# A residual block with forgetting attention: who issues the forget-row loads, where four weight splits stand, and where two output projections begin

## The chip, the cores and the metric

The kernel runs on one core of one Trainium2 chip. The metric is the device time of one execution in microseconds (us), median of the runs. Five engines work side by side: PE (TensorE, matmuls), DVE (VectorE), ACT (ScalarE), POOL (GpSimd) and SP (SyncE, which here only issues DMAs). Each takes its instructions strictly in order; they meet through semaphores, and a wait holds back everything behind it on the same engine.

## The reference, cut to what matters

```python
h = rms_norm(x, g1);  z = h @ w_in                  # x: 512 tokens x 1024 channels
q, k = rms_norm(q), rms_norm(k)                      # per head, 8 heads of 64
F = cumsum(log_sigmoid(z_f + b))                     # forget rows, one per head
s = q @ k.T * d**-0.5 + F[t] - F[s], causal;  y_attn = softmax(s) @ v
y_pool = pool_scale * ((trailing_mean(z_pool, w) - z_pool) @ w_pool[g])   # w = 2, 4, 8, 16
x = x + concat[y_pool, y_attn] @ w_out               # the mixer stage ends here
x = x + peer_ffn(rms_norm(x, g2))                    # 128 x 128 experts, top 16 of 8 heads
```

## The kernel before

**Layout.** Channels lie on the 128 partitions, the 512 tokens along the free dimension. Every weight block is one of a numbered list n = 0, 1, 2, ...: 0 to 3 are the value projections, 4 is the forget projection (`F_W`), 5 to 12 the query and key projections (`QK_W`), 13 to 16 the pool projections (`POOL_W`), 17 to 24 the output projections (`OUT_W`), 25 to 28 four early expert blocks (`EARLY_W`), and from 29 on the retrieval queries and the experts.

**A weight's way.** Matmuls are made in pairs of parts, high and low, so each block is loaded by SP into one of three buffers `raw` (L392), ACT copies the high part to `wh` (`hi_to`, L438, called "split n" below), POOL subtracts to get the low part `wl` (L411), and PE's projection n (`project`, L620 to L622, 24 matmuls of 512 columns) waits for `w_lo`. SP may load block n once the low part of n - 3 is done; ACT may split n once projection n - 4 has used its buffer. In the mixer stage ACT calls `hi_to(n + 3)` at projection n, just before it copies that projection's result to `zc` (L473). The first norm calls `hi_to` at k = 1 and k = 7 (splits 0 and 1), its second half at k = 0 and 4 (splits 2 and 3). The second norm has split 28 at k = 4; splits 29 to 32 come in the stage after it.

**The order of the mixer stage** is written out by hand in `stages`, one list that PE follows with what stands inside each projection, and that ACT and DVE follow flattened (`in_turn`). `head(h, n, more)` stands for the transposes of head h's probabilities, projection n, and inside it at given k: the sums of squares and norm of an earlier q or k (`ss`, `norm`), the four score blocks of head h + 1 (`score`, PE L705; DVE L1017 to L1022; ACT's exponential L491) and their scaling (`scale`, L1030), and head h's last transposes. `pv` is the product with the values. Each head has one forget row, broadcast over the partitions into `nf[h % 2]`, which DVE adds to the scores (L1019).

**The forget rows** come from DVE's scan (L960, semaphore `f_done`). SP stores them to memory (L372), waits for the store, and loads row h with `nf` (L379) ahead of weight block `SCORED[h]` + 1, that is ahead of blocks 9, 10, 12, 13, 14, 15, 16 and 17. For h of 2 and more it first waits for `s_masked` = 4(h - 1): that the last score block of head h - 2 has been masked by DVE, since this frees the buffer.

**Pool mixing.** DVE makes the trailing mean of group g (`mean`, L984 to L1001), PE multiplies it by `w_pool` (`poolmix`, L695), ACT and DVE store high and low parts to `hh` and `hl` (L486, L1005). All four products use one bank, `bank[SS]`, so a poolmix waits for the one before to be stored (`pool_lo`).

**The end of the stage.** Output projection 17 has the order k = 4, 5, 6, 0, 1, 2, 3, 7, as the pool parts (k below 4) and the last pair of heads (k = 7) come last. Each output projection is added to x by DVE (L965), and its square sum is taken one projection later (L635).

## Time and profile before

| what | us |
|---|---|
| runs shown: median (lowest to highest) | 1580.68 (1578.74 to 1581.0) |
| the profiled execution: its own time | 1589.65 |
| its span, first to last instruction | 1587.8 |
| PE busy, share of the span | 1521.5, 96% |
| DVE busy | 1148.2, 72% |
| POOL busy | 973.5, 61% |
| ACT busy | 604.8, 38% |

In the profile a row of an engine's timeline is "start us, duration us, engine, line, instruction, count", and in brackets how long the engine had been idle before it and what ended that idle time. PE is drawn as busy over nearly the whole span, but in the first 300 us, the mixer stage and the second norm, its slices show seven to eight tenths, and the granted TensorE clock is below full speed in several of them. From there to the end the slices are at nine tenths and more.

### The profile page before, as it was taken

How to read it: one execution, taken by the hardware profiler on the slowest of the kernel's cores; microseconds unless marked ns; L12 is line 12 of the kernel's file. 1: busy time of each engine (PE TensorE's matmuls, PEld its weight loads, DVE VectorE, ACT ScalarE, POOL GpSimd, SP SyncE). 2: the span in 40 equal slices, each digit the busy share in tenths (PEclk: the TensorE clock that was granted, in tenths of full speed). 3: DMA queues.
4: the chain of work that ended last, by engine and by line, in shares of the span. 5: the costliest groups of instructions: out<-in, count | busy, mean ns of one | idle time of the engine just before them, and what ended most of it. 6: DMA issues, size and time to landing. Idle time of an engine off the chain costs nothing.

```text
span 1587.8 us, 20624 instructions
## 1 busy us (share of the span) xinstructions
PE 1521.5 (96%) x7613; PEld 1326.5 (84%) x7613; DVE 1148.2 (72%) x1938; ACT 604.8 (38%) x808; POOL 973.5 (61%) x525
## 2 busy tenths in 40 slices
PE   7888889899999999999999999999999999999999
PEld 4654557788999999999999999998888888888887
DVE  5565572416699999928898889938777777777774
ACT  5565433433333333343343334433333333333332
POOL 2411113333468788667666676658787878878784
PEclk9998899999999999999999999999999999999999
DMA  4211212222347777658989988799889888888983
GB/s 152 94 40 40 79 41 80 99 81 80 113 168 267 266 255 269 216 174 303 346 310 355 363 337 317 254 325 392 338 336 350 319 349 318 345 343 326 349 303 119
DMA packets 117973, 381.52 MB, mean 240 GB/s; under 512 B 11416, under 2 KB 27928, under 8 KB 117408
## 3 DMA queue, kind: packets, MB, share of 16 engines
q1 hardware_dynamic: 71264, 204.76, 35.5%
q0 software_dynamic: 36864, 134.23, 23.1%
q10 hardware_dynamic: 9792, 41.95, 6.6%
q8 instruction: 18, 0.29, 0.1%
q14 instruction: 35, 0.29, 0.0%
HBM read 336.84 MB, written 44.06 MB: 240 GB/s over the span
## 4 chain that ended last, share of the span: by engine, by line
PE 81%; DVE 6%; DMA 5%; ACT 4%; issue 2%; POOL 1%; SPq 0%; ACTq 0%; DVEq 0%
PE bank L620 25%; PE bank L621 25%; PE bank L622 24%; PE bank L809 5%; DMA picked<-u_dram,picks 3%; DMA raw<-wst_dram 2%; PE bank L753 1%; POOL wl L411 1%; DVE zc L933 1%; ACT wh L438 1%; DVE rinv L916 1%; PE bank L705 1%; ACT L509 1%; PE bank L635 1%; ACT L511 0%
## 5 line engine op out<-in xcount | busy, mean ns | idle before, releaser
L411 POOL TENSOR_TENSOR wl<-raw,wh 128x1024 fp32r<-128x1024 f32 x211 | 521.3, 2472 | 488.4 <-ACT wh L438 487.3
L620 PE MATMUL bank<-hh,wh 128*128 128x384 f32 (+1 forms) x1184 | 427.0, 361 | 4.2 <-POOL wl L411 4.2
L621 PE MATMUL bank<-hl,wh 128*128 128x384 f32 (+1 forms) x1184 | 414.1, 350 | 0.0
L622 PE MATMUL bank<-hh,wl 128*128 128x384 f32 (+1 forms) x1184 | 413.9, 350 | 0.0
L438 ACT ACTIVATE wh<-raw 128x1024 fp32r<-128x1024 f32 x225 | 237.0, 1054 | 172.3 <-PE bank L622 138.9
L621 PE MATMUL bank<-wl,Wh 128*128 128x512 f32 x768 | 300.7, 392 | 0.0
L620 PE MATMUL bank<-wh,Wh 128*128 128x512 f32 x768 | 300.0, 391 | 0.0
L622 PE MATMUL bank<-wh,Wl 128*128 128x512 f32 x768 | 298.4, 389 | 0.0
L620 PEld LDWEIGHTS bank<-hh,wh 128*128 128x128 f32 x1184 | 224.7, 190 | 14.1 <-issue 6.2
L621 PEld LDWEIGHTS bank<-hl,wh 128*128 128x128 f32 x1184 | 224.8, 190 | 9.6 <-issue 1.7
L622 PEld LDWEIGHTS bank<-hh,wl 128*128 128x128 f32 x1184 | 224.0, 189 | 8.9
L421 POOL DMA_INDIRECT picked<-v_dram,picks x128 | 195.3, 1526 | 24.9 <-issue 22.2
L1046 DVE SCALAR_TENSOR_TENSOR junk<-picked,wide 128x1024 bf16<-128x1024 f32 x128 | 155.2, 1213 | 25.2 <-DMA picked<-u_dram,picks 23.1
L620 PEld LDWEIGHTS bank<-wh,Wh 128*128 128x128 f32 x768 | 144.2, 188 | 31.8
L622 PEld LDWEIGHTS bank<-wh,Wl 128*128 128x128 f32 x768 | 144.2, 188 | 31.1
L621 PEld LDWEIGHTS bank<-wl,Wh 128*128 128x128 f32 x768 | 144.3, 188 | 29.2
L1173 DVE SCALAR_TENSOR_TENSOR wide<-picked,pick_a,wide 128x1024 f32<-128x1024 f32 x128 | 163.7, 1279 | 0.5
L411 POOL TENSOR_TENSOR wl<-xraw,wh 128x1024 fp32r<-128x1024 f32 x54 | 131.3, 2432 | 49.9 <-ACT wh L438 49.3
L438 ACT ACTIVATE wh<-xraw 128x1024 fp32r<-128x1024 f32 x72 | 76.7, 1066 | 198.2 <-PE bank L622 182.9
L560 ACT ACTIVATE act_a<-bank 128x384 f32<-128x384 f32 x124 | 61.1, 493 | 232.5 <-PE bank L622 224.7
L421 POOL DMA_INDIRECT picked<-u_dram,picks x128 | 125.4, 979 | 30.3 <-issue 19.6
L1152 DVE TENSOR_TENSOR oh<-bank,slotT 128x1024 f32<-128x1024 f32 x96 | 117.4, 1223 | 34.8 <-ACT bank L577 31.2
(164 smaller groups left out, 1767.2 us busy)
## 6 DMA issues: line engine op xcount, KB each, us to landing
raw<-uT_dram SPq DMA_DIRECT2D x128, 512.0 KB
xraw<-v_dram SPq DMA_DIRECT2D x72, 512.0 KB
raw<-v_dram SPq DMA_DIRECT2D x56, 512.0 KB
a_dram<-act_a ACTq DMA_DIRECT2D x64, 384.0 KB
wf<-a_dram SPq DMA_DIRECT2D x32, 768.0 KB, 6.9
raw<-wst_dram SPq DMA_DIRECT2D x41, 512.0 KB
gates_dram<-gbuf ACTq DMA_DIRECT2D x4, 4096.0 KB, 16.6
gt<-gates_dram SPq DMA_DIRECT2D x32, 512.0 KB
```

Of the source, the lines that this page charges most:

```text
L411: pool.tensor_tensor(wl[:, n % SPLIT, :], raw_of(n), wh[:, n % SPLIT, :].bitcast(F32), ALU.subtract).then_inc(w_lo, 1)
L421: pool.indirect_dma_start(out=picked[:, j % ROWS, :], out_offset=None, in_=u if j < PICKS else v_rows, in_offset=bass.IndirectOffsetOnAxis ...
L438: act.activation(wh[:, n % SPLIT, :], raw_of(n), ACT.Copy).then_inc(w_hi, 1)
L509: act.activation(root[:, :], var[:, :], ACT.Ln).then_inc(ln_ready, 1)
L560: act.activation(a_of(j), bank[n % 2][:, 0:DT], ACT.Gelu).then_inc(out_done, 1)
L620: pe.matmul(dst, ah, bh, start=start, stop=False)
L621: pe.matmul(dst, ah, bl, start=False, stop=False)
L622: return pe.matmul(dst, al, bh, start=False, stop=stop)
L809: last = pe.matmul(bank[GP + of % 2][:, t * P:(t + 1) * P], oh[:, of % 2, 1, t, :], oh[:, of % 2, 0, t, :], start=True, stop=True)
L1046: dve.scalar_tensor_tensor(junk[:, :], picked[:, j % ROWS, :], 1.0, wide[:, :], ALU.mult, ALU.mult, accum_out=pick_a[:, j:j + 1]).then_inc ...
L1152: step(dve.tensor_tensor(oh[:, s], bank[IOTA_BANK][:, 0:P].unsqueeze(1).unsqueeze(1).broadcast_to(both), slotT[:, 0:2, at].unsqueeze(3).br ...
L1173: dve.scalar_tensor_tensor(wide[:, :], picked[:, j % ROWS, :], pick_a[:, i:i + 1], wide[:, :], ALU.mult, ALU.add).then_inc(first_added, 1)
```

## The change

- SP no longer stores or loads the forget rows. ACT does: it waits for `f_done` and issues the store between the copy of projection 5 to `zc` and its square; it waits for the store and issues the rows of heads 0 and 1 in the same place of projection 6; and after the last exponential of head h it issues the row of head h + 2, with no wait of its own.
- ACT splits weight 1 at k = 4 of the first norm and weight 2 at k = 7; weights 28, 29 and 30 at k = 0, 3 and 6 of the second.
- `begin` is new: the nine matmuls of k = 4, 5, 6 of output projections 17 and 18 are issued before poolmix 2 and after mean 3. The projections then run k = 0, 1, 2, 3, 7.
- poolmix 1 moves from k = 6 to k = 0 of projection 16, ahead of head 7's scores.

```diff
-        stages += head(6, POOL_W + 3, (6, "mean", 2), (6, "poolmix", 1)) + [("pv", 6, [])]
-        stages += [("poolmix", 2, []), ("transpose", (7, 0), []), ("transpose", (7, 1), []), ("mean", 3, [])]
-        stages += [("transpose", (7, 2), []), ("pv", 7, []), ("poolmix", 3, [])]
+        stages += head(6, POOL_W + 3, (0, "poolmix", 1), (6, "mean", 2)) + [("pv", 6, [])]
+        stages += [("begin", OUT_W, []), ("poolmix", 2, []), ("transpose", (7, 0), []), ("transpose", (7, 1), [])]
+        stages += [("mean", 3, []), ("begin", OUT_W + 1, []), ("transpose", (7, 2), []), ("pv", 7, [])]
+        stages += [("poolmix", 3, [])]
...
+        BEGUN, LEFT = (4, 5, 6), (0, 1, 2, 3, 7)
...
-                if n == SCORED[0] + 1:
-                    sp.wait_ge(f_done, 1)
-                    sp.dma_start(f_dram, fg[:, 2, :]).then_inc(f_stored, 16)
-                    sp.wait_ge(f_stored, 16)
-                for h in range(HEADS):
-                    if n != SCORED[h] + 1:
-                        continue
-                    if h >= 2:
-                        sp.wait_ge(s_masked, TB * (h - 1))
-                    sp.dma_start(nf[:, h % 2, :], f_dram[h:h + 1, :].broadcast_to([P, T])).then_inc(nf_in[h % 2], 16)
...
+            def forget(h):
+
+                act.dma_start(nf[:, h % 2, :], f_dram[h:h + 1, :].broadcast_to([P, T])).then_inc(nf_in[h % 2], 16)
+
...
-                        if k in (1, 7):
-                            hi_to(k // 7)
+                        if k in (1, 4, 7):
+                            hi_to(k // 3)
...
+                        if n == QK_W[0]:
+                            act.wait_ge(f_done, 1)
+                            act.dma_start(f_dram, fg[:, 2, :]).then_inc(f_stored, 16)
+                        elif n == QK_W[1]:
+                            act.wait_ge(f_stored, 16)
+                            for h in range(2):
+                                forget(h)
...
+                    if b == TB - 1 and h + 2 < HEADS:
+                        forget(h + 2)
...
-                        if what == "norm2" and k in (0, 4):
-                            hi_to(EARLY_W + 2 + k // 4)
+                        if what == "norm2" and k in (0, 3, 6):
+                            hi_to(EARLY_W + 3 + k // 3)
...
+            def free_bank(n):
+
+                if bank_of(n) in last_in_bank:
+                    pe.wait_ge(*taken(last_in_bank[bank_of(n)]))
+                last_in_bank[bank_of(n)] = n
...
+                    begun = n in (OUT_W, OUT_W + 1)
                     project(bank[bank_of(n)][:, :], n % SPLIT, *((hh, hl) if kd == "out" else (mh, ml)), between,
-                            (4, 5, 6, 0, 1, 2, 3, 7) if n == OUT_W else range(KD))
+                            LEFT if begun else range(KD), first=BEGUN[0] if begun else 0)
...
+                elif what == "begin":
+                    pe.wait_ge(w_lo, i + 1)
+                    free_bank(i)
+                    project(bank[bank_of(i)][:, :], i % SPLIT, hh, hl,
+                            lambda k: pe.wait_ge(att_lo, 2 * (k - 4) + 2), BEGUN, first=BEGUN[0])
```

## Rows read from the trace of the kernel before

**Rows 1.** Chain that ended last, first 300 us, shares of the whole span by line:

```profile
by line: PE bank L620 8.6%; DMA raw<-wst_dram 8.3%; PE bank L621 8.0%; PE bank L622 8.0%; issue 7.2%; DVE zc L933 3.7%; DVE rinv L916 3.2%; PE bank L705 3.0%; ACT L509 3.0%; PE bank L635 2.8%; ACT L511 2.6%; DVE pr L1019 2.5%; DVE pad L989 
```

**Rows 2.** Waits, 120 to 190 us: who <- for whom, us in total, times, longest:

```profile
ACT wh L438 <- DMA raw<-wst_dram: 18.1, 4, 5.4
```

**Rows 3.** Waits of SP's queue, first 300 us, same columns:

```profile
SPq L379 <- DVE nmax L1022: 111.0, 6, 23.4
```

**Rows 4.** Timeline of SP's queue, one of six such pairs:

```profile
144.54 0.33 SPq L379 DMA_DIRECT2D nf<-forget_dram  x1
144.91 0.43 SPq L392 DMA_DIRECT2D raw<-wst_dram  x1
```

**Rows 5.** Timeline of ACT: one split, last exponentials of heads 5, 6 and 7:

```profile
149.64 1.06 ACT L438 ACTIVATE wh<-raw 128x1024 fp32r<-128x1024 f32 x1 [4.28 <-DMA raw<-wst_dram]
...
180.51 0.72 ACT L491 ACTIVATE pr<-pr,nmax 128x512 f32<-128x512 f32 x1 [0.81 <-DVE nmax L1022]
...
199.14 0.72 ACT L491 ACTIVATE pr<-pr,nmax 128x512 f32<-128x512 f32 x1 [4.28 <-DVE nmax L1022]
...
214.03 0.73 ACT L491 ACTIVATE pr<-pr,nmax 128x512 f32<-128x512 f32 x1 [2.07 <-DVE nmax L1022]
```

**Rows 6.** Windows: length, busy PE, PEld, DVE, ACT, POOL, granted clock, DMA, GB/s:

```profile
126.14:144.54 18.40, 13.94 (x46) 7.93 (x47) 9.66 (x31) 10.37 (x19) 2.35 (x1) 0.91 0.13 43
...
155.00:164.00 9.00, 9.00 (x17) 4.80 (x16) 6.67 (x23) 4.83 (x12) 0.00 (x0) 0.50 0.02 8
```

**Rows 7.** Timeline of PE: scores of heads 6 and 7, poolmix 2:

```profile
182.69 0.92 PE L705 MATMUL bank<-kn,qn 64*128 64x128 f32 x4
...
205.74 0.92 PE L705 MATMUL bank<-kn,qn 64*128 64x128 f32 x4
...
222.06 1.84 PE L695 MATMUL bank<-pm,wp 128*128 128x512 f32 x2 [4.05 <-DVE hl L1005]
```

**Rows 8.** Timeline of DVE: means 1 and 2, first steps of poolmix 0 and 1, x of projection 18:

```profile
200.60 0.42 DVE L984 COPY pad<-zc 128x512 f32<-128x512 f32 x1
...
205.58 0.74 DVE L1005 SCALAR_TENSOR_TENSOR hl<-bank,vec,hh 128x512 fp32r<-128x512 f32 x1
...
215.49 0.42 DVE L984 COPY pad<-zc 128x512 f32<-128x512 f32 x1
...
221.17 0.74 DVE L1005 SCALAR_TENSOR_TENSOR hl<-bank,vec,hh 128x512 fp32r<-128x512 f32 x1
...
242.20 0.69 DVE L965 TENSOR_TENSOR x<-x,bank 128x512 f32<-128x512 f32 x1 [2.92 <-PE bank L622]
```

**Rows 9.** Timeline of PE: first matmuls of projections 1, 3 and 4:

```profile
24.98 0.80 PE L620 MATMUL bank<-wh,hh 128*128 128x512 f32 x1 [2.93 <-POOL wl L411]
...
39.41 0.50 PE L620 MATMUL bank<-wh,hh 128*128 128x512 f32 x1 [0.32 <-POOL wl L411]
...
46.81 0.50 PE L620 MATMUL bank<-mh,wh 128*128 128x512 f32 x1 [1.19 <-POOL wl L411]
```

**Rows 10.** Timeline, DVE's scan and PE's first two sums of squares of q and k:

```profile
58.27 3.25 DVE L960 TENSOR_TENSOR_SCAN fg<-fg 8x512 f32<-8x512 f32 x1
59.43 1.10 PE L635 MATMUL bank<-sq,cst 128*128 128x512 f32 x2 [1.44 <-ACT sq L443]
...
70.73 2.04 PE L635 MATMUL bank<-sq,cst 128*128 128x512 f32 x2 [4.72 <-ACT sq L443]
```

**Rows 11.** Timeline, second norm: ACT's split 28, DVE's last parts, PE's projection 29:

```profile
294.75 1.06 ACT L438 ACTIVATE wh<-raw 128x1024 fp32r<-128x1024 f32 x1 [0.76 <-DVE zc L933]
...
300.95 1.48 DVE L869 TENSOR_TENSOR hl<-zc,hh 128x512 fp32r<-128x512 f32 x2
...
307.02 0.47 PE L620 MATMUL bank<-hh,wh 128*128 128x512 f32 x1 [4.22 <-POOL wl L411]
```

**Rows 12.** Timeline of ACT and of its queue, early expert blocks:

```profile
304.72 1.06 ACT L438 ACTIVATE wh<-raw 128x1024 fp32r<-128x1024 f32 x1
304.86 0.34 ACTq L531 DMA_DIRECT2D a_dram<-act_a  x1
```

## What the change will do to the time, predicted before it ran

> **What bounds the kernel now.** I read the slices of the page first: from about 300 us on PE is at nine tenths and above, so an edit of the first 300 us acts by how much earlier the retrieval queries start, and the rest moves along with them. I find no wait there that this change touches. Then the chain that ended last, for those 300 us. Three PE lines of the projections hold most, but the fourth entry is the transfer of weight blocks, 8.3% [rows 1]. So PE is not the only bound here. The waits say whose it is: from 120 to 190 us ACT stands four times before split 14, 15, 16 and 17 for a transfer, 18.1 us in all, 5.4 the longest [rows 2]. Why is the transfer late? SP stood 111.0 us before its loads of forget rows, on DVE's mask [rows 3], and the weight load is issued right behind: row at 144.54, block 15 at 144.91 [rows 4], split at 149.64 after 4.28 of idling [rows 5]. Its buffer had been free for long. Two heads, from the mask at 144.54 to the last exponential of head 5 at 180.51, take 35.97 us, 18.0 each [rows 4, 5].
>
> **Part 1, the rows on ACT's queue, heads 3 to 5.** SP now waits only for a free buffer, so blocks 14 to 17 are there long before they are split, and the four waits go. What is late next? In a head's 18.4 us PE is busy 13.9 at a mean clock of 0.91, DVE 9.7, ACT 10.4 [rows 6]. PE's work at full clock is 13.9 x 0.91 = 12.7. Without its wait a head takes 18.0 - 4.3 = 13.7 (splits, copies, table loads, exponential, DVE's norm steps, the next scores, one after another). That is still above 12.7, so the chain through ACT and DVE stays the bound, by 1 us, and three waits come back whole: 18.1 - 5.35 = **-12.8**.
> The rows themselves: each is issued behind an exponential of 0.72 us [rows 5] and takes ACT's sequencer 0.34. The trace has such an issue on ACT, at 304.86, beside a split that started at 304.72 [rows 12]: the engine doesn't stop. I take 0; were none hidden, 6 x 0.34 = 2.0. What the row waits for, the mask, the exponential ahead of it has waited for already, and it is wanted over a head's time later, so its own transfer is covered.
>
> **Head 6.** Its scores start at 182.69, behind transposes that wait for DVE, which stays so. From there PE ran into 5.35 us of waiting and then half clock. Head 7's scores started at 205.74 with PE never idle, and the exponential came 8.3 us later, at 214.03 [rows 5, 7]. By that pattern head 6's comes at 182.69 + 8.3 = 191.0, not 199.14 [rows 5]: **-8.2**, of which 5.35 is the wait and the rest clock.
>
> **Head 7, with poolmix 1 moved ahead of its scores.** It needs mean 1 and the stored parts of poolmix 0. DVE needs 205.58 - 200.60 = 5.0 for the mean [rows 8] and starts it 1.5 after the exponential: 191.0 + 1.5 + 5.0 + 0.7 = 198.2. PE gets there at 195.7: after the exponential it still has 1.7 of projection and poolmix 0, the value product (2.16) and the transposes (0.86), 4.7 in all. So it stands 2.5, where before it never stood. Head 7's last exponential follows 0.45 + 8.3 later, 206.95, a period of 16.0 for 14.9: **+1.1** (0 if the mean comes sooner, +3.5 if the stand drops the clock).
>
> **The tail.** Before: exponential 214.03 to x of projection 18 at 242.20, 28.2 [rows 5, 8], with PE idle 4.05 before poolmix 2 alone [rows 7], as poolmix 1's parts were stored only at 221.9 [rows 8]. After, from 206.95: value product until 210.0, begin 17 (9 matmuls, 0.233 from one start to the next at full clock, 2.1) until 212.1. Poolmix 2 waits for mean 2, 1.5 + 5.7 [rows 8] after the exponential, 214.2. Transposes to 215.6, begin 18 to 217.7, the last transposes and value product to 220.8; mean 3 (4.5) ends at 221.2; poolmix 3; then 15 + 15 matmuls, 7.0, end at 228.9: 22.0. **-6.2**. The 18 matmuls moved are 4.2 of it; the others are poolmix 1's earlier store. Poolmix 2 and mean 3 keep a stand of 2.0 and 0.4. Bounds: -3 (half clock after these stands) to -8.
>
> **Part 2, splits 1 and 2 earlier.** Projection 1 started at 24.98, waiting for POOL; now at 22. But projection 3 waits for split 3, which doesn't move (39.41), and projection 4 for split 4 (46.81) [rows 9]. So nothing is gained, and the idle time gathers before projection 3: 39.4 - 22 - 2 x 5.5 = 6.4 us. After the 2.9 us at 24.98 two projections took 14.1 us for 11, as the clock fell [rows 9]: a loss of 3.1, unseen then. It now falls in projection 3, with 1.2 us of slack behind it: +1.9 (0 to +4). The split inside the norm's alternation of ACT and DVE costs 0.3 (0 to 1.06).
>
> **Part 3, the store of the rows on ACT.** The wait for the scan stands between the copy of projection 5 and its square; behind it on ACT are the square, the root of that norm, split 9, and POOL, PE and DVE wait for those. The scan ends at 61.5, the square's sum ran on PE at 59.43 [rows 10]. Now it is 61.5 + 0.34 + 0.65, near 62.6: +3.1, with PE idle 4.7. Against it, PE's idle of 4.72 before the next sum at 70.73 [rows 10] goes for the most part (ACT stood for block 9, held on SP by the rows). The two idles change places, one projection earlier, each with a spell of half clock behind it. Following kn to the first scores I get -1.0 for the pair. Parts 2 and 3 together: **+1.2**, with bounds -2.5 and +5.
>
> **Part 4, second norm.** Before, projection 29 waited for POOL until 307.02, 4.22 us, since its split came only after the norm [rows 11]. Now splits 28 to 30 stand in the norm. Each takes 1.06 in a gap of 0.76 [rows 11], so 0.3 late, and at k = 0 there is no gap, 1.0; less the old one, 1.3 in all. The norm's last low part was done at 302.4 [rows 11], so projection 29 starts near 303.7: **-3.3** (-1.5 to -4.2). What now ends last is DVE's norm.
>
> **Sum.** 1.2 - 12.8 - 8.2 + 1.1 - 6.2 - 3.3 = **-28.2 us**. The profiled execution took 1589.65 with a span of 1587.8, which the sum makes 1559.6; the median of the runs shown is 9 below it, and the difference lies outside the stage. 1580.7 - 28.2 = **1552.5**.
>
> **A rule against it.** SP's queue shows that the weight load was held by a wait of 111.0 us, not by transfers: a row and a block are issued 0.37 us apart [rows 3, 4]. That speaks for order, not bandwidth, as the bound.
> The Trainium skill (DMA: Bandwidth & Descriptors, section Issuing engines are not separate DMA queues) states that DMAs from several engines share the same 16 DMA engines, and that spreading them saves only the issue time. By that rule alone the first rival below is the outcome, 1571. I hold that the rule tells of transfers, not of the in-order wait in front of them.
>
> **Rivals.**
> *Only the issues come back (0.03).* If the blocks were late for transfer time rather than for SP's place, part 1 returns 6 x 0.37 = 2.2 [rows 4] for 21, and the sum is -9: 1571. For it: a block needs 4.7 us to land [rows 4, 5]. Against: by the code its buffer was block 12's, split a whole head before, and the DMA share is 0.13 [rows 6].
> *The clock takes part of it (0.22).* PE's margin per head is 1 us; in 155 to 164 us it was at 0.50 with PE busy throughout [rows 6]. One head at half clock lasts about as long as 12.7 / 0.5 = 25.4 by PE alone, partial spells cost 2 to 4 each; two or three of them at head 7's poolmix, in the tail and at the start: 1556 to 1563.
> *No spells at all (0.20).* Heads packed closer leave PE little idle, projections 3 and 6 run at full clock: 1546 to 1550.
> *Slower (0.02).* If tight heads leave PE just idle enough to be held at the half level from head 2 to head 7, a head takes 25.4 for 13.7, 11.7 more. From 28.2 / 11.7 = 2.4 such heads on the change loses; with four it ends at 1580.7 - 28.2 + 46.8 = 1599. Against: the fuller heads of now (199 to 214) ran at full clock nearly throughout.
> *Forecast, 1550 to 1556 (0.53).*
>
> **Range and chances.** The range 1545 to 1562 holds the forecast, the case without spells and most of the case with them. About 0.2%, 3.2 us, is what a measurement of this kernel can tell from no change. All cases but the slower one lie beyond it on the fast side, less 0.01 for two heads at half clock, which end near no change: faster 0.97, same 0.01, slower 0.02.
>
> **What would show it.** Right: no row "ACT wh <- DMA raw" after 72 us; a head's period near 13.8; SP waiting on POOL only; PE idle about 2.5 before poolmix 1 and 2 before poolmix 2; projection 29 started by DVE's last `hl`, some 28 us before 307. Wrong: first sum of squares of q not 3 us late (part 3), projection 4 within 0.5 of 46.8 (part 2), heads of 15 us and more with PE as the releaser or half clock (the margin of 1 us), ACT idle behind a row's issue.

## The result and the profile after

The changed kernel takes 1562.78 us (median of 6 runs, 1558.53 to 1571.51), the kernel before took 1580.84 beside it (6 runs, 1578.74 to 1584.26). The ratio is 0.9894, with a 95% interval of 0.9872 to 0.9916: 1.1% faster, some 17 to 18 us, where 28.2 were forecast. The median lies 0.8 us above the top of the range.

The profiled execution of after took 1571.51, with a span of 1569.7, against 1589.65 and 1587.8. Both profiles lie about 9 us above their medians, so they can be set side by side. The page of after:

```profile
PE 1513.6 (96%) x7613; PEld 1323.5 (84%) x7613; DVE 1156.7 (74%) x1938; ACT 602.9 (38%) x808; POOL 973.6 (62%) x525
```

From 1587.8 to 1569.7 PE gave back 8 us of busy time, with the same matmuls: that is clock (mean granted clock 0.983, before 0.978). DVE's busy time has **risen** by 8.5 us, though it has no new work. That line is the first trace of what I missed.

The same points of the stage in both traces give the shift of each stretch, to be set against the forecast. Each step is the change of one stretch, in us:

| stretch, its end before → after | before | after | measured | forecast |
|---|---|---|---|---|
| start to projection 4, 46.81 → 47.02 | 46.81 | 47.02 | +0.2 | +2.2 |
| to exponential of head 0, 88.82 → 89.65 | 42.01 | 42.63 | +0.6 | -1.0 |
| heads 1 and 2, 126.14 → 126.95 | 37.32 | 37.30 | 0.0 | 0 |
| heads 3 to 5, 180.51 → 168.17 | 54.37 | 41.22 | -13.15 | -12.8 |
| head 6, 199.14 → 182.13 | 18.63 | 13.96 | -4.7 | -8.2 |
| head 7, 214.03 → 198.78 | 14.89 | 16.65 | +1.8 | +1.1 |
| tail, to x of projection 18, 242.20 → 222.99 | 28.17 | 24.21 | -4.0 | -6.2 |
| x of projection 18 to x of 24, 280.92 → 261.71 | 38.72 | 38.72 | 0.0 | 0 |
| second norm, to projection 29, 307.02 → 288.01 | 26.10 | 26.30 | +0.2 | -3.3 |
| from there to the end of the span | 1280.8 | 1281.7 | +0.9 | 0 |

So 19.0 of 28.2 arrived at projection 29. The waits show that part 1 did what was said. SP's queue, first 300 us, against the 111.0 on DVE in [rows 3]; the same view of ACT from 120 to 200 us holds no wait of `wh` for a transfer, against [rows 2]:

```profile
SPq L382 <- POOL wl L401: 278.9, 33, 17.4
```

The last exponentials of heads 2, 5, 6 and 7 in ACT's timeline, with the issue of a forget row beside one of them (against [rows 5]):

```profile
126.95 0.72 ACT L492 ACTIVATE pr<-pr,nmax 128x512 f32<-128x512 f32 x1 [0.81 <-DVE nmax L1037]
...
168.17 0.72 ACT L492 ACTIVATE pr<-pr,nmax 128x512 f32<-128x512 f32 x1 [0.81 <-DVE nmax L1037]
168.18 0.33 ACTq L437 DMA_DIRECT2D nf<-forget_dram  x1
...
182.13 0.72 ACT L492 ACTIVATE pr<-pr,nmax 128x512 f32<-128x512 f32 x1 [3.84 <-DVE nmax L1037]
...
198.78 0.72 ACT L492 ACTIVATE pr<-pr,nmax 128x512 f32<-128x512 f32 x1 [2.07 <-DVE nmax L1037]
```

Head 2's, at 126.95, is the point from which the three heads are counted. All six such issues (heads 0 to 5) stand beside the exponential, 0.33 us beside 0.72, and cost nothing, as [rows 12] had it. Windows of after, with the columns of [rows 6]: head 5, head 6, head 7, the tail, and the second norm.

```profile
154.78:168.17 13.39, 13.05 (x53) 7.95 (x52) 9.67 (x31) 9.60 (x19) 2.35 (x1) 1.00 0.17 59
168.17:182.13 13.96, 12.10 (x42) 7.23 (x41) 10.26 (x31) 5.75 (x14) 2.38 (x1) 0.81 0.18 58
182.13:198.78 16.65, 15.49 (x58) 9.34 (x57) 12.36 (x34) 7.37 (x16) 2.67 (x1) 0.95 0.09 32
198.78:222.99 24.21, 21.42 (x84) 15.56 (x83) 15.86 (x28) 9.31 (x15) 5.30 (x3) 0.93 0.12 44
264.28:288.01 23.73, 16.61 (x96) 16.29 (x95) 19.27 (x22) 12.00 (x16) 7.29 (x3) 0.96 0.14 47
```

Heads 3 to 5 run at full clock and take 14.05, 13.77 and 13.39 us. From head 6 on the clock is below it, and DVE has more busy time than its steps need: 10.26 in head 6 against 8.19 before.

**Where the rest went.** The chain that ended last, in after, goes through one long piece in head 6 (start, length, what):

```profile
170.08 2.86 DVE pad L1004
```

and the timeline around it:

```profile
170.01 2.38 POOL L401 TENSOR_TENSOR wl<-raw,wh 128x1024 fp32r<-128x1024 f32 x1 [11.04 <-ACT wh L428]
170.08 2.85 DVE L1004 TENSOR_TENSOR pad<-pad 128x512 f32<-128x512 f32 x1
...
175.54 0.88 PE L720 MATMUL bank<-kn,qn 64*128 64x384 f32 x2 [1.65 <-DVE nmax L1037]
```

One addition of mean 0 takes 2.85 us. In before the same addition took 0.69:

```profile
182.42 0.69 DVE L989 TENSOR_TENSOR pad<-pad 128x512 f32<-128x512 f32 x1
...
187.81 2.34 POOL L411 TENSOR_TENSOR wl<-raw,wh 128x1024 fp32r<-128x1024 f32 x1 [16.48 <-ACT wh L438]
```

The difference is what POOL does meanwhile. In after it subtracts block 17 from 170.01 to 172.39, and DVE's step, begun 0.07 later, ends 0.5 behind it (172.93). In before split 17 was late for its transfer, so POOL came at 187.81, when all of mean 0 was over. This was my theory after the result, **A**: a DVE step that reads two operands from SBUF stands until a running subtraction of POOL ends. The early splits, which part 1 makes possible and part 4 orders, put POOL's subtractions on top of such steps. The Trainium skill (SBUF — State Buffer, section Who interferes with whom) states this: a DVE instruction with two SBUF inputs contends with a GpSimd instruction that reads SBUF, this contention is an exclusive lock on the ports that the two share, and the order of issue decides who blocks. The trace agrees, 0.69 against 2.85 with POOL's row begun 0.07 ahead; I had not used that rule in the prediction.

The second norm has three of them. Its low parts (`hl`) on DVE, all eight (ns: least/median/most), and the splits 28 to 30 on POOL beside the long ones:

```profile
L884 DVE TENSOR_TENSOR hl<-zc,hh x8: 678/686/2551, 272.2 to 287.3; 128x512 fp32r<-128x512 f32 x8
```

```profile
271.72 2.39 POOL L401 TENSOR_TENSOR wl<-raw,wh 128x1024 fp32r<-128x1024 f32 x1 [11.16 <-ACT wh L428]
272.20 2.47 DVE L884 TENSOR_TENSOR hl<-zc,hh 128x512 fp32r<-128x512 f32 x1 [0.99 <-ACT hh L526]
...
278.02 2.48 POOL L401 TENSOR_TENSOR wl<-raw,wh 128x1024 fp32r<-128x1024 f32 x1 [3.90 <-ACT wh L428]
278.49 2.55 DVE L884 TENSOR_TENSOR hl<-zc,hh 128x512 fp32r<-128x512 f32 x1 [0.26 <-ACT hh L526]
...
284.38 2.42 POOL L401 TENSOR_TENSOR wl<-raw,wh 128x1024 fp32r<-128x1024 f32 x1 [3.89 <-ACT wh L428]
284.86 3.10 DVE L884 TENSOR_TENSOR hl<-zc,hh 128x512 fp32r<-128x512 f32 x2 [0.25 <-ACT hh L526]
...
288.01 0.80 PE L623 MATMUL bank<-hh,wh 128*128 128x512 f32 x1 [7.12 <-DVE hl L884]
```

The trace of before had one such pair of rows in this norm, and I read over it:

```profile
295.90 2.41 POOL L411 TENSOR_TENSOR wl<-raw,wh 128x1024 fp32r<-128x1024 f32 x1 [16.12 <-ACT wh L438]
296.37 2.49 DVE L869 TENSOR_TENSOR hl<-zc,hh 128x512 fp32r<-128x512 f32 x1 [0.26 <-ACT hh L523]
```

### The profile page after: what moved, and what is told of

Its sections match the earlier page's. It is cut to its first block, busy times and chain, and to the rows that moved or that the text cites. A ratio compares the mean times of both kernels' runs of the same rounds, so it can differ in the third digit from the quotient of the medians.

```text
span 1569.7 us, 20625 instructions
## 1 busy us (share of the span) xinstructions
PE 1513.6 (96%) x7613; PEld 1323.5 (84%) x7613; DVE 1156.7 (74%) x1938; ACT 602.9 (38%) x808; POOL 973.6 (62%) x525
## 4 chain that ended last, share of the span: by engine, by line
PE 79%; DVE 7%; ACT 5%; DMA 5%; issue 4%; POOL 1%; ACTq 0%; SPq 0%; DVEq 0%
PE bank L623 24%; PE bank L624 24%; PE bank L625 24%; DMA picked<-u_dram,picks 4%; PE bank L824 4%; ACT wh L428 1%; PE bank L768 1%; POOL wl L401 1%; DVE rinv L931 1%; DVE hl L884 1%; PE bank L639 1%; ACT L512 1%; DVE pr L1034 1%; DVE pad L1004 1%; PE bank L720 1%
## 5 line engine op out<-in xcount | busy, mean ns | idle before, releaser
L623 PEld LDWEIGHTS bank<-hh,wh 128*128 128x128 f32 x1184 | 225.3, 190 | 17.1 <-DVE hl L884 7.4
```

Of the source, the lines that this page charges most:

```text
L623: pe.matmul(dst, ah, bh, start=start, stop=False)
```

## The experiments

Letters in the expectations stand for readings of the same loss: A is the one above, the others are told in each. "After" is the changed kernel, from which each kernel differs only by the edit shown; each ratio is against the kernel before, run on the same chip, and after's own is 0.9894 (0.9872 to 0.9916). "By the ratios" is the difference from 0.9894, of 1580 us; as each interval is about 0.25% wide to either side, such a difference is good to some 5 us. Where a stretch is given, it is from one profiled execution of each kernel.

### The second norm

**Splits as before.**

```diff
-                        if what == "norm2" and k in (0, 3, 6):
-                            hi_to(EARLY_W + 3 + k // 3)
+                        if what == "norm2" and k in (0, 4):
+                            hi_to(EARLY_W + 2 + k // 4)
```

> The changed kernel with one part undone: in the second norm only split 28, at k = 4, as before. In the changed kernel each of the three splits there is followed by a DVE step L884 of 2.5 us for 0.69. Theory A (such a step of DVE, with two inputs in SBUF, stands until POOL's subtraction of 2.4 us is over): one such step instead of three, so the norm's last low part comes 4.8 us sooner after its start, PE's projection 29 starts when POOL's low part of block 29 is there, about where it does now: total within 1 us of the changed kernel (1562.8), some 18 below the kernel before. Theory of the prediction (splits cost ACT 1.3, the wait for POOL is worth 4.2): 3.3 us slower than the changed kernel.

Measured: 1560.38 us, ratio 0.9863 (0.984 to 0.9887). From x of projection 24 to projection 29 it takes 26.1 us (262.51 to 288.61), in after 26.3. Part 4 bought nothing: in after projection 29 no longer waits for POOL, but for a norm that ends 23.7 us after its variance instead of 18.9 as here.

**POOL held back until the low parts are done**, the splits of ACT left where after has them:

```diff
                     pool.wait_ge(w_hi, n + 1)
+                    if n == EARLY_W + 3:
+                        pool.wait_ge(h_lo, 2 * KD)
```

> The changed kernel, but POOL subtracts block 28 (and so all after it) only once the second norm's last low part is done. Nothing on DVE or ACT changes in the norm; all three splits on ACT stay. Theory A (POOL's subtraction holds DVE steps with two SBUF inputs): the three L884 steps of 2.5 us become 0.69, from the norm's var to its last low part it takes 19 to 19.5 us instead of 23.7, though the end gets later by the three subtractions now behind it (about 5 us slower in total). Rival B (the long steps are DVE's own, at fixed places of its program, as for loading instructions): they stay at 2.5 us at the same places, 23.7 us.

Measured: 1567.99 us, one run only; that is 5.2 above after's median, about what was expected, though one run can't show it. ACT's and DVE's instructions are those of after, in their order; only POOL starts later. The eight low parts, and POOL's row:

```profile
L886 DVE TENSOR_TENSOR hl<-zc,hh x8: 684/686/693, 273.4 to 283.0; 128x512 fp32r<-128x512 f32 x8
```

```profile
283.86 9.53 POOL L403 TENSOR_TENSOR wl<-raw,wh 128x1024 fp32r<-128x1024 f32 x4 [22.11 <-DVE hl L886]
```

No step is longer than 0.693, and from the variance to the last low part it takes 18.2 us (265.47 to 283.7), in after 23.7. So A holds here: 5.5 us are POOL's doing, and the reading by which the steps are long of themselves, or from ACT's splits, fell. It also sizes the splits on ACT: the norm with the splits of before takes 18.9, with one hold of 1.8 in it, so 17.1 without; three splits make 18.2 of it. That is 1.1 us for the 1.3 of the prediction.

**Split 29 right behind the norm**, splits 27 and 28 as before:

```diff
+                if what == "early":
+                    hi_to(EARLY_W + 4)
                     for j in range(UP_EARLY):
```

> The changed kernel with the second norm's splits as before (28 at k = 4), and split 29 moved to straight behind the norm, ahead of the first Gelu. Theory A: POOL gets block 29 1.7 us sooner than before, and only one DVE step in the norm is held: from the x of projection 24 to PE's projection 29 it takes 24.3 us for 26.3 now and 26.1 before; 2 us faster than the changed kernel (2.0 to 4 by medians with their noise).

Measured: 1557.62 us, 0.9855 (0.9833 to 0.9877). Projection 29 starts 24.3 us after x of projection 24 (263.19 to 287.52), 2.0 less than in after, and waits for POOL for 0.94 instead of the 4.22 of before ([rows 11]):

```profile
287.52 0.47 PE L624 MATMUL bank<-hh,wh 128*128 128x512 f32 x1 [0.94 <-POOL wl L401]
```

Two of the 3.3 us forecast can be had with a split that stands behind the norm's DVE steps and not among them.

### Heads 6 and 7

**Splits 17, 18 and 19 later**, behind copies of the transposed probabilities, where DVE's mean is over:

```diff
-                    if n >= 2:
+                    if n >= 2 and n not in (14, 15, 16):
                         hi_to(n + 3)
...
                                    ACT.Copy).then_inc(pt_saved, 1)
+                    if i in ((5, 1), (6, 1), (7, 2)):
+                        hi_to(12 + h)
```

> The changed kernel with splits 17, 18 and 19 moved on ACT: after the copies of the next transposes (17, 18) and after the last transposes of head 7 (19), so that POOL's subtractions don't meet means 0, 1 and 2 on DVE. Same work in all. Theory A: means 0, 1 and 2 lose their long steps (2.1 each): head 6's exponential comes 2 to 4 us sooner, as PE then doesn't stand 1.65 before its scores, and the poolmixes follow; in all 5 to 8 us faster than the changed kernel. Rival B (DVE's own): long steps stay, 0 +- 1. Rival C (the 2.7 us missing in head 6 are the half clock by itself, not DVE's late masks): 0 +- 2, with the half clock still at head 6.

Measured: 1554.84 us, 0.9832 (0.9807 to 0.9858), by the ratios 9.8 us under after; from head 5's last exponential to x of projection 18 it takes 47.8 us, in after 54.8, 7.0 less. Head 6, head 7 and the tail:

```profile
169.72:180.21 10.49, 10.32 (x45) 6.47 (x43) 8.12 (x31) 5.88 (x14) 2.38 (x1) 1.00 0.24 75
180.21:194.84 14.63, 14.10 (x57) 8.73 (x56) 10.34 (x34) 7.27 (x17) 2.38 (x1) 1.00 0.11 38
194.84:217.51 22.67, 20.13 (x84) 14.36 (x83) 15.87 (x28) 9.41 (x15) 5.26 (x3) 1.00 0.14 47
```

```profile
171.63 0.69 DVE L1006 TENSOR_TENSOR pad<-pad 128x512 f32<-128x512 f32 x1
```

POOL's busy time is the same, but the mean's addition is back at 0.69, and the clock is 1.00 in all three windows. Head 6 takes 10.49, in after 13.96; the forecast had 10.5 (191.0 less 180.51). So the loss in head 6 begins with 2.2 us of DVE standing, which lets PE stand for 1.65 before the next scores, and behind that PE was at half clock: in after from 177 to 184 us PE was busy throughout at a granted clock of 0.52.

The two can be told apart. In the kernel "squares ahead", further down, head 6 has the same instructions, the same hold of mean 0 (2.85 us at 166.14) and the same stand of PE, but no half clock:

```profile
164.22:176.41 12.19, 10.32 (x45) 6.42 (x43) 10.28 (x31) 5.76 (x14) 2.38 (x1) 1.00 0.18 65
```

```profile
171.60 0.88 PE L720 MATMUL bank<-kn,qn 64*128 64x384 f32 x2 [1.66 <-DVE nmax L1037]
```

Head 6 takes 12.2 us there, and 12.2 with a clock of 1.00 in the kernel with splits 9, 10 and 13 moved too. So of the 3.5 us the hold alone is 1.7 (12.2 less 10.5) and the half clock 1.8 (14.0 less 12.2). The stand of PE made the spell possible and not certain.

**poolmix 1 back at k = 6**, behind head 7's scores:

```diff
-        stages += head(6, POOL_W + 3, (0, "poolmix", 1), (6, "mean", 2)) + [("pv", 6, [])]
+        stages += head(6, POOL_W + 3, (6, "mean", 2), (6, "poolmix", 1)) + [("pv", 6, [])]
```

> The changed kernel with poolmix 1 back at k = 6 of projection 16; the begun projections stay. Theory of the prediction: head 7 gets 1.1 us shorter, as PE doesn't stand for mean 1, but poolmix 2 then waits for poolmix 1's parts behind mean 2: 0.7 us later than now, so 0 to 1.5 us faster or slower in all. Rival C (PE's stand in front of poolmix 1 costs a spell of half clock): head 7's period falls from 16.7 to 14.9 or less, and 2 us or more faster.

Measured: 1564.66 us (4 runs), 0.9866 (0.9844 to 0.9888). The interval overlaps after's; the windows say more:

```profile
182.38:196.93 14.55, 14.55 (x56) 8.95 (x54) 11.70 (x33) 6.68 (x16) 2.53 (x1) 0.93 0.11 38
196.93:220.19 23.26, 20.72 (x87) 14.85 (x86) 16.40 (x30) 9.86 (x16) 5.34 (x3) 1.00 0.13 46
```

Head 7 takes 14.55 instead of 16.65, so the move of poolmix 1 costs 2.1 there, as forecast in kind. The tail takes 23.26 instead of 24.21, but at a clock of 1.00 for 0.93. Four other kernels ran after's tail at 1.00 and took 22.65 to 22.68 us: those with the second norm's splits undone, with POOL held back, with part 1 undone and with part 2 undone. The first of them:

```profile
201.11:223.79 22.68, 19.93 (x84) 14.30 (x83) 15.85 (x29) 9.30 (x15) 5.31 (x3) 1.00 0.14 47
```

At the same clock the move gives the tail 0.6 us back, where the forecast counted about 2 for the earlier store.

**Both begins behind poolmix 3**, so that nothing is begun beside head 7:

```diff
-        stages += [("begin", OUT_W, []), ("poolmix", 2, []), ("transpose", (7, 0), []), ("transpose", (7, 1), [])]
-        stages += [("mean", 3, []), ("begin", OUT_W + 1, []), ("transpose", (7, 2), []), ("pv", 7, [])]
-        stages += [("poolmix", 3, [])]
+        stages += [("poolmix", 2, []), ("transpose", (7, 0), []), ("transpose", (7, 1), []), ("mean", 3, [])]
+        stages += [("transpose", (7, 2), []), ("pv", 7, []), ("poolmix", 3, [])]
+        stages += [("begin", OUT_W, []), ("begin", OUT_W + 1, [])]
```

> The changed kernel with both begun parts (18 matmuls of projections 17 and 18) issued after poolmix 3 and not in the gaps before poolmix 2 and after mean 3. Theory of the prediction: they cost their 4.2 us again, 3.5 to 4.2 us slower. Rival D (the second begun part, 3.5 us at half clock in the profile of the changed kernel, stands in front of head 7's last transposes and value product, so most of what it saves is paid there): 0.5 to 2 us slower only.

Measured: 1572.51 us, 0.9917 (0.9897 to 0.9937). The tail:

```profile
198.37:226.13 27.76, 22.35 (x84) 15.63 (x83) 15.82 (x28) 9.51 (x15) 5.26 (x3) 0.88 0.11 38
```

27.76 against 24.21: 3.55 us in the profiles, and 3.6 by the ratios, where the prediction counted 4.2 as moved matmuls and rival D 0.5 to 2. The size fits the prediction's. It isn't proven: the clock differs as well, 0.88 for 0.93, and the intervals of the two ratios overlap.

### The rows and the first 90 us

**Part 1 undone**: SP stores and loads the rows again, everything else as in after.

```diff
+                if n == QK_W[3] + 1:
+                    sp.wait_ge(f_done, 1)
+                    sp.dma_start(f_dram, fg[:, 2, :]).then_inc(f_stored, 16)
+                    sp.wait_ge(f_stored, 16)
+                for h, at in enumerate((9, 10, 12, 13, 14, 15, 16, 17)):
+                    if n != at:
+                        continue
+                    if h >= 2:
+                        sp.wait_ge(s_masked, TB * (h - 1))
+                    sp.dma_start(nf[:, h % 2, :], f_dram[h:h + 1, :].broadcast_to([P, T])).then_inc(nf_in[h % 2], 16)
... (and ACT's store and its calls of forget go)
```

> The changed kernel with part 1 alone undone: the forget rows are stored and loaded on SP again, ahead of the same weight blocks as before. Theory of the prediction: ACT waits for blocks 14 to 17 again, 12.8 us in heads 3 to 5 and what head 6 loses; the square's sum is not held any more. 14 to 18 us slower than the changed kernel, near 1579. Rival (the gain came from the other parts): within 4 us of the changed kernel.

Measured: 1583.9 us (10 runs), 0.9992 (0.9978 to 1.0005). All that the change gained is gone: 0.9992 less 0.9894 is 0.98%, 15.5 us, and x of projection 18 comes at 238.44, 15.4 later than in after. The waits from 72 to 200 us and SP's queue, to be set beside [rows 2] and [rows 3]:

```profile
ACT wh L438 <- DMA raw<-wst_dram: 19.1, 4, 5.5
```

```profile
SPq L379 <- DVE nmax L1038: 111.6, 6, 23.3
```

The same transfers through the same memory, with only the place of a small store and eight small loads changed: it is the order on SP's queue, not bandwidth. The rival "only the issues come back" (1571) would have left 2.2 us here.

**Squares ahead of ACT's wait for the scan** and of its row issues:

```diff
+                        if kind(n) == "qk":
+                            act.wait_ge(zc_ready, z + 1)
+                            square(SQ_QK + z, zc[:, z % 2, :])
                         if n == QK_W[0]:
                             act.wait_ge(f_done, 1)
...
-                        if kind(n) == "qk":
-                            act.wait_ge(zc_ready, z + 1)
-                            square(SQ_QK + z, zc[:, z % 2, :])
```

> The changed kernel with the forget rows' issues on ACT put behind the squares of projections 5 and 6, so that the wait for the scan doesn't hold the square. The theory of part 3 (the square's sum is 3.1 us late for that wait, PE stands 4.7 and falls to half clock): the sum comes back to 59.6 us, the wait for block 9 stays away, the first exponentials of head 0 come 4 to 7 us sooner, and all behind it: 4 to 6.5 us faster than the changed kernel. Rival (ACT and DVE absorb it, as the norm's root waits for DVE behind the scan anyway): under 1.5 us.

Measured: 1557.02 us, 0.9855 (0.9829 to 0.988), by the ratios 6.2 us under after. PE's first sums of squares, here and in after:

```profile
58.93 0.67 PE L639 MATMUL bank<-sq,cst 128*128 128x512 f32 x1 [1.44 <-ACT sq L433]
...
66.93 0.67 PE L639 MATMUL bank<-sq,cst 128*128 128x512 f32 x1 [1.44 <-ACT sq L433]
```

```profile
62.82 1.19 PE L639 MATMUL bank<-sq,cst 128*128 128x512 f32 x1 [4.65 <-ACT sq L433]
...
73.47 0.67 PE L639 MATMUL bank<-sq,cst 128*128 128x512 f32 x1 [1.75 <-ACT sq L433]
```

The first sum comes 3.9 us sooner and the second 6.5, and the exponential of head 0 comes at 85.69, not 89.65. Of each 0.7 was there at projection 4 already (46.33 for 47.02), where the two kernels are the same; so ACT's wait for the scan costs head 0 3.3 us, a little under the 4 to 7 expected. The prediction saw this wait and let block 9's earlier load pay for it; without the wait both are had.

**Splits of the first norm as before**, part 2 undone:

```diff
-                        if k in (1, 4, 7):
-                            hi_to(k // 3)
+                        if k in (1, 7):
+                            hi_to(k // 7)
```

> The changed kernel with the splits of the first norm as before (0 at k = 1, 1 at k = 7). Theory A: in the changed kernel POOL meets DVE at 18.2 us in the norm's first half (a step of 1.95) and not after the root any more (before: 2.75 at 27.9), so the two differ by under 1 us where projection 4 starts, 46.8 for 47.0; PE's idle of 4.8 and its half clock before projection 3 go back before projection 1, where nothing waits. Within 1.5 us of the changed kernel. Theory of the prediction: the change cost 1.9 + 0.3 here, so undone it is 2.2 us faster.

Measured: 1560.74 us, 0.9864 (0.9841 to 0.9887). Projection 4 starts at 46.73, in after at 47.02, in before at 46.81. PE's idle time has the places that the prediction gave it: 2.92 before projection 1 and 1.78 before projection 3 here,

```profile
24.92 0.80 PE L623 MATMUL bank<-wh,hh 128*128 128x512 f32 x1 [2.92 <-POOL wl L401]
```

and all of it before projection 3 in after:

```profile
38.72 0.79 PE L623 MATMUL bank<-wh,hh 128*128 128x512 f32 x1 [4.83 <-POOL wl L401]
```

By the table part 2 costs 0.2 to 0.3 us, not 2.2, and even that isn't shown: among the other kernels, which have after's splits in the first norm, projection 4 starts anywhere from 46.05 to 47.25. The ratio would give 4.7, which no stretch of the trace that this edit touches has.

**Splits 9, 10 and 13 behind the squares.** After's Newton steps of the q and k norms (`rinv`, 0.69) met POOL too: three of the eight took 2.7 or more.

```diff
-                    if n >= 2:
+                    if n >= 2 and n not in (6, 7, 10):
                         hi_to(n + 3)
...
                             square(SQ_QK + z, zc[:, z % 2, :])
+                            hi_to(n + 3)
```

> The changed kernel with splits 9, 10 and 13 behind the squares of projections 6, 7 and 10 on ACT, so that POOL doesn't subtract while DVE makes the three newton steps that stood 2.77, 2.77 and 2.73 us. Theory A: each is 0.69 again; the split now costs ACT up to 1 us ahead of a root; 3 to 5 us faster than the changed kernel. Rival B: the steps stay long, 0 to 2 us slower.

Measured: 1560.6 us, 0.9882 (0.9859 to 0.9906). The long steps are gone,

```profile
69.07 0.69 DVE L932 SCALAR_TENSOR_TENSOR rinv<-newt,root 128x512 f32<-128x512 f32 x1
```

but the exponential of head 0 comes at 89.95 (89.65 in after) and that of head 2 at 126.17 (126.95): 0.8 us sooner, not the 3 to 5 expected, and projection 4 was 0.9 sooner already (46.16 for 47.02). A miss: in this kernel three holds of 2 us taken off DVE bring nothing that the trace shows. It is not so in general. The first combination below has the same move together with the squares ahead; set against the kernel with only the squares ahead, with projection 4 at 46.33 in both, its exponential of head 0 comes at 82.75 for 85.69 and that of head 2 at 118.97 for 122.99, 4.0 us, as much as expected. Why the move pays only beside the other wasn't taken apart.

### What the parts give together

**First combination:** the squares first, splits 9, 10 and 13 behind them, splits 17 to 19 later, and the second norm as before with split 29 right behind it. The diffs of these four stand above; the two on `hi_to(n + 3)` become one:

```diff
-                    if n >= 2:
+                    if n >= 2 and n not in (6, 7, 10, 14, 15, 16):
                         hi_to(n + 3)
```

> The changed kernel with what the first runs point to: squares ahead of the rows' issues (5.8 us by its own run), splits 17 to 19 clear of the means (8.0), split 28 at k = 4 and split 29 straight after the second norm; and new, splits 9, 10 and 13 behind the squares, so that POOL doesn't meet the three newton steps that stood 2.1 each. Theory A: the parts add up, 5.8 + 8.0 + 1.7 + 3 to 6 = 18 to 21 us faster than the changed kernel, near 1543. Rival B for the new part (those three long steps are DVE's own): they stay, and the sum is 15, near 1548.

Measured: 1547.95 us, 0.9772 (0.9752 to 0.9793). By the ratios that is 19 us under after, inside the 18 to 21 of theory A; in the traces projection 29 starts 15.4 sooner (272.58 for 288.01). The long Newton steps are gone, against rival B.

**Second combination:** the same with poolmix 1 back at k = 6, and split 19 left to the next call of `hi_to`, at projection 17 together with split 20, behind poolmix 3.

```diff
-                    if i in ((5, 1), (6, 1), (7, 2)):
+                    if i in ((5, 1), (6, 1)):
...
-        stages += head(6, POOL_W + 3, (0, "poolmix", 1), (6, "mean", 2)) + [("pv", 6, [])]
+        stages += head(6, POOL_W + 3, (6, "mean", 2), (6, "poolmix", 1)) + [("pv", 6, [])]
```

> The first combination with two more edits: poolmix 1 back at k = 6 of projection 16 (the profile of that kernel alone had the stretch from head 5's last exponential to the x of projection 18 at 51.6 us for 54.8) and split 19 only behind poolmix 3, since it met a step of mean 3 (2.86 us for 0.69). Theory A: 3 + 1 to 2 us faster than the first combination, a ratio of 0.974 to 0.975 to the kernel before. Rival C (poolmix 1's place matters only by the clock, and the combination has hardly any half clock left): within 1 us of the first combination.

Measured: 1539.62 us (1534.8 to 1541.02), 0.9741 (0.972 to 0.9762): 2.6% under the kernel before and, by the ratios, 24 us under after and 4.9 under the first combination, as theory A had it; in the traces projection 29 starts 4.8 sooner. Head 6, head 7 and the tail:

```profile
160.03:170.53 10.50, 10.33 (x45) 6.48 (x43) 8.12 (x31) 5.89 (x15) 2.38 (x1) 1.00 0.25 75
170.53:183.53 13.00, 13.00 (x55) 8.27 (x53) 9.67 (x33) 6.69 (x16) 2.38 (x1) 1.00 0.13 42
183.53:205.81 22.28, 21.70 (x90) 15.39 (x89) 16.25 (x29) 9.71 (x16) 4.77 (x2) 1.00 0.10 30
```

Full clock throughout. Head 7 takes 13.00 for 14.62 in the first combination, both at a clock of 1.00, so poolmix 1's place isn't only a matter of clock (rival C); PE is busy for 13.00 of the 13.00, so it is the bound there. Projection 29 starts at 267.78, in after at 288.01.

## Why the prediction was right and where it failed

**Part 1, heads 3 to 5: right.** -13.15 for -12.8, and undoing part 1 gives back 15.5 us of the kernel's time, so the rows carry nearly all of the gain. The estimate of 13.7 us for a head was met (14.05, 13.77 and 13.39). The row's issue on ACT at nothing was right too.

**Head 6: the step that failed is "by that pattern head 6's comes at 182.69 + 8.3".** The pattern took DVE's mean 0 at the length it had in before, 0.69 for its addition, which was so short only because split 17 was late. The early split 17 is itself what part 1 brings. Measured -4.7 for -8.2; with POOL out of the way 10.49 for the forecast 10.5. Of the 3.5 missing the hold is 1.7 and the half clock behind it 1.8. (The "5.35 us of waiting" in that passage is ACT's wait; PE itself was idle for 4.03.)

**Part 4: the step that failed is "so 0.3 late" and "1.3 in all".** I costed the splits on ACT, where they stand in a gap, and not POOL's subtraction that each one starts. The 1.3 itself was right (1.1). The term that is missing is three holds of DVE, 5.5 us, where before had one of 1.8: 1.1 + 5.5 - 1.8 = 4.8 later, which eats the 4.6 us that projection 29 stood behind the last low part (302.4 to 307.02), and the stretch ends at +0.2 for -3.3. I followed the moved split on ACT and on SP's queue, not on POOL.

**Head 7 and the tail: kind right, size off.** Head 7 +1.8 for +1.1. PE stood 1.16 before poolmix 1 and 2.21 before poolmix 2, where 2.5 and 2.0 were forecast:

```profile
189.46 0.67 PE L710 MATMUL bank<-pm,wp 128*128 128x512 f32 x1 [1.16 <-DVE hl L1020]
...
206.20 0.70 PE L710 MATMUL bank<-pm,wp 128*128 128x512 f32 x1 [2.21 <-DVE pm L1016]
```

The times of the means, "5.0" and "5.7" from [rows 8], contain holds by POOL already. These rows are from before:

```profile
203.24 2.21 DVE L998 TENSOR_TENSOR pm<-pad,cst 128x16 f32<-128x16 f32 x1
...
215.94 4.17 DVE L989 TENSOR_TENSOR pad<-pad 128x512 f32<-128x512 f32 x3
```

A step of 16 columns takes 2.21 us where the same step of mean 0 takes 0.17, and three additions take 4.17 for 3 x 0.69. They were taken as the work of the mean, when they were a wait that a moved split removes. After has the same holds in its means 1 and 2 (2.21 and 2.85 us), so they explain no difference of after from before; mean 0's is new. The tail's forecast was 22.0 us. At full clock it takes 22.65 to 22.68 (four kernels), so of the 2.2 missing 1.5 is clock, 0.93 in after, and 0.65 is size: poolmix 1's earlier store is worth 0.6, not 2. Head 7's +1.8 is the mildest case: in five of the eight other kernels with the same head 7 it took 18.2 to 19.8 us (last section), at or beyond the forecast's bound of "+3.5 if the stand drops the clock".

**Parts 2 and 3: the sum of +1.2 came out at +0.8 from two terms that were both off.** Part 2 was sized at +2.2 and cost 0.2: projection 3 did run at half clock for most of its length and took 2.3 us longer (not 3.1), but it began 0.7 sooner, and the slack of 1.2 behind it took the rest but for 0.2 to 0.4. The pair of part 3 was sized at -1.0 and cost 0.6. The first sum of squares was 3.4 late for 3.1.

**The rivals.** The measured median lies where the rival "the clock takes part of it" (1556 to 1563, 0.22) ends. Its place is right, head 6 to the tail, and half-clock spells are what PE shows there. But it took them to come from heads packed too closely; they followed stands of PE, and in head 6 the stand followed DVE's hold. Closer heads without the holds ran at full clock (the two combinations), which is the case "no spells at all" for heads 6 and 7. "Only the issues come back" is excluded by the kernel with part 1 undone, "slower" by the result itself. The range missed because it held no mechanism on the engines that the splits set going.

**Left open.** By the ratios, undoing part 4, part 2 or the move of poolmix 1 each gains 0.3%, with intervals that overlap after's. After's own six runs reach from 1558.5 to 1571.5, so some of that 0.3% may be after's spread and not the parts; I take those terms from the traces. After wasn't run again on the chips of the other kernels, so each difference of ratios holds the spread of two chips. Why the same stand of PE is followed by half clock in one execution and not in another stays open. Nor was the dose tried (a subtraction of twice the length on POOL). The rest of the span after projection 29 took between 1265 and 1282 us over the profiles, with all but the same instructions; its cause is open. Of the 36.7 us by which the second combination's span is shorter than after's, 20.2 lie ahead of projection 29 and the rest there, so the ratio of medians is the fairer figure for it.

## What to carry to other kernels

When a split, a copy or a load is moved, follow it to the last engine that it sets going: the gain of an early weight was right on ACT and SP, and was eaten by the subtraction on POOL that each split starts, on top of a norm's DVE steps. Ahead of any sum of durations, look in the trace of before for instructions of one line and shape whose longest is three times the median: that can be a wait inside an instruction, as here, which no view of waits shows, and a moved neighbour makes it come or go. A load that must wait for compute goes on the queue of the engine that does or sees that compute, not in front of loads that are free to go, and not ahead of work that its engine could still do.

## What the runs showed of the hardware

- A DVE step with two operands in SBUF stands until a subtraction of 128 x 1024 on POOL, begun before it, is over: 0.69 us becomes 2.5 to 2.85, a step of 16 columns 2.21 for 0.17. Steps that read a PSUM bank and began under such a subtraction kept their length within 0.04 us, ahead of 310 us in before and after (`hl<-bank,hh`: 0.67 to 0.70). One step with a single tile and a column of scalars was held too, 1.43 for 0.47 us, where no time was lost by it:

```profile
223.72 1.43 DVE L907 TENSOR_SCALAR zc<-x,vec 128x512 f32<-128x512 f32 x1
```

- The profile books this as busy time of DVE: it rose by 8.5 us over the span, with 1938 instructions in both kernels, and no row of the waits names it. Counted against the shortest step of its line and shape, ahead of 310 us, before has eight held steps with 15.3 us in all and after thirteen with 23.5: 8.2 of the 8.5.
- Head 7 with the same instructions on every engine took 16.65 us in after and 19.77 in the kernel with the second norm's splits undone, at granted clocks of 0.95 and 0.83; nothing ahead of head 7 differs between the two. DVE's hold fell on other steps of the mean, of about the same sum (3.45 us for two additions there, 2.21 for the step of 16 columns in after). DVE's row and the window of head 7 in the kernel with the second norm's splits undone:

```profile
183.25 3.45 DVE L1004 TENSOR_TENSOR pad<-pad 128x512 f32<-128x512 f32 x2
```

```profile
181.34:201.11 19.77, 17.23 (x57) 10.68 (x56) 12.36 (x34) 7.38 (x16) 2.41 (x1) 0.83 0.08 28
```

Over all profiles with this head 7 it took 16.65 to 16.69 us in four, 18.20 in two and 19.76 to 19.79 in three. So a stretch with stands of 1 to 2.5 us on PE carries some 3 us of chance from one execution to the next, and a step read from one profile there is no better than that.
